# Hi products first, then lo products, in the merged up groups of a split-precision MLP

## The chip, the cores and the metric

The kernel runs on one core of a Trainium2 chip. The metric is device time in microseconds for one execution; lower is better. Before the change the median of three runs is 1174.59 us (1173.49 to 1175.37).

## The reference, cut to what matters

One decoder layer over 256 tokens with a width of 2048, all in float32: modulated norm, combined projection, two kinds of attention and a convolution, output projection, then the MLP, which is the part that the change touches:

```python
h = rms_norm(x, norm2_g[l]) * (1.0 + sc2) + sh2
x = x + g2 * (jnp.square(jax.nn.relu(h @ w_mlp1[l])) @ w_mlp2[l])   # 2048 -> 8192 -> 2048
return rms_norm(x, final_g)
```

## The kernel before

Every large product is computed from two parts of each operand: a rounded copy (hi, type fp32r) and what is left of it (lo). For `h @ w` three products are summed: hi x hi, hi x lo, lo x hi. The weights come from memory as float32 blocks (`raw`, four buffers, 1 MB each, two "halves" in a block). For each half of 128 x 1024 weights, the scalar engine (ACT) writes the rounded copy into `w_hi[j % 4]` (`weight_hi`, line 893) and counts `hi_done`; the vector engine (DVE) subtracts it from the raw weights into `w_lo[j % 4]` (`weight_lo`, line 1850) and counts `lo_done`; TensorE (PE) multiplies the half and counts `pe_half` at its last product. SyncE refills a raw block once `lo_done` says that it was used. The cast of half j waits for `pe_half` of half j - 4, because there are four buffers.

The activations of the MLP's first matrix, h, lie in `act_both` (line 319) as 16 blocks of 128 features, each with 256 tokens of hi and then 256 tokens of lo.

The MLP goes through four quarters of the 8192 hidden features. The first quarter's first matrix is done with three narrow products (`feature_rows`, lines 1275 to 1277). In quarters 1, 2 and 3 it is done by `up_group` and `merged_rows` (lines 1280 to 1311): four groups a quarter, 512 hidden features each, over 8 halves. A half has two blocks of 128 input features (kk) and four tiles of 128 hidden features (m), each tile with a PSUM bank of its own in `quad[par]`. For each kk and m there is one *wide* product (line 1285: 128 weight columns of w_hi, and hi and lo of the activations side by side, 512 columns) and one *narrow* product (line 1287: w_lo with the hi activations, 256 columns, added to the first half of the same bank). So a half has 8 wide and 8 narrow products in turn, and in the whole kernel there are 12 groups, 96 halves and 768 of each. The groups of a quarter are run by a loop of two passes over two groups (`mlp_up`, line 1798), in which thresholds of waits depend on the loop's register.

Each quarter then has four down groups (`down_group`, `split_group`), in which the weights are the moving operand of 512 columns (`token_rows`, lines 1299 to 1301), and some halves of which (`split_half`, lines 1329 to 1357) are replaced by 21 narrow products with waits for sums of weights and activations.

Of the kernel before, what the change touches and what calls it, by code (L numbers as in the profile page):

```python
# [7 lines left out]
P = 128  # L8
D = 2048
S = 256  # L10
TT = S // P
KT = D // P
# [12 lines left out]
GW = 512  # L25
# [6 lines left out]
HALVES = 8  # L32
# [207 lines left out]
def build(nc, x_d, c_d, wmod_d, bcol_d, bmod_d, n1_d, n2_d, fg_d, main_d, tail_d, bf_d, wck_d, wcv_d, pos_d,  # L240
# [7 lines left out]
    with ctx:  # L248
        def sb(name, shape, dt=f32, where=ctx):
            return where.enter_context(nc.sbuf_tensor(name, shape, dt))  # L250

        def sem(name):
            return ctx.enter_context(nc.semaphore(name))
# [3 lines left out]
        w_hi = [sb(f"w_hi{i}", [P, 2 * GW], f32r) for i in range(4)]  # L257
        w_lo = [sb(f"w_lo{i}", [P, 2 * GW], f32r) for i in range(4)]
# [56 lines left out]
        def in_hold(name, start, shape, dt=f32):  # L315
            return nc.alloc_sbuf_tensor_at(name, shape, dt, offset=hold_at + start)

        K = 1024
        act_both = in_hold("act", 0, [P, KT, 2, S], f32r)
        act_hi, act_lo = act_both[:, :, 0, :], act_both[:, :, 1, :]  # L320
# [92 lines left out]
        quad = [ctx.enter_context(nc.psum_tensor(f"quad{i}", [P, 4 * GW], f32)) for i in range(2)]  # L413
# [20 lines left out]
        hi_done = sem("hi_done")  # L434
        lo_done = sem("lo_done")
        pe_half = sem("pe_half")
# [828 lines left out]
        def _(pe):  # L1265
            mm = nc.tensor.matmul
# [10 lines left out]
                    last = mm(out, lo, act_hi[:, k, :], start=False, stop=end, skip_group_check=True)  # L1277
                return last

            def merged_rows(par, j, k, kk, begin, end):  # L1280

                for m in range(4):
                    out = quad[par][:, m * GW:(m + 1) * GW]
                    cols = slice(kk * GW + m * P, kk * GW + (m + 1) * P)
                    mm(out, w_hi[j % 4][:, cols], act_both[:, k, :, :].rearrange("p h t -> p (h t)"),  # L1285
                       start=begin, stop=False, skip_group_check=True)
                    last = mm(out[:, 0:S], w_lo[j % 4][:, cols], act_hi[:, k, :], start=False, stop=end,  # L1287
                              skip_group_check=True)
                return last

            def token_rows(par, j, k, kk, a_hi, a_lo, begin, end, width=GW, tiles=range(TT), weights=None):
# [12 lines left out]
            def up_group(g, par):  # L1304

                for j in range(HALVES):
                    pe.wait_ge(lo_done, g * 8 + (j + 1))
                    for kk in range(2):
                        k = 2 * j + kk
                        last = merged_rows(par, j, k, kk, k == 0, k == KT - 1)  # L1310
                    last.then_inc(pe_half, 1)

            def down_group(q, cg, gates=False):

# [105 lines left out]
            for k in range(KT):  # L1420
                one = mm(quad[0][:, k * P:(k + 1) * P], c_act[:, k:k + 1].to_broadcast([P, P]), ident[:, :],
                         start=True, stop=True)
# [200 lines left out]
            for slot, (half, step) in enumerate(SLOTS):  # L1623
# [42 lines left out]
                if slot == NSA_SLOT + 3:  # L1666
                    pe.wait_ge(cmp_sb, 2)
                    for g in range(NKV):
                        last = nc.tensor.transpose(spare[:, P + g * HD:P + (g + 1) * HD], v_cmp_t[:, g, :],
                                                   ident[0:HD, 0:HD])  # L1670
# [5 lines left out]
                if slot in (NSA_SLOT + 11, NSA_SLOT + 12):  # L1676
# [4 lines left out]
                    for g in range(NKV):  # L1681
                        last = nc.tensor.transpose(
                            spare[:, g * P:(g + 1) * P],
                            p_cmp[:, tt, 4 * g:4 * g + 4, :].rearrange("p h n -> p (h n)"), ident[:, :])
# [113 lines left out]
            def mlp_up(q):  # L1798
                with pe.Fori(0, 2) as i:
                    for par in range(2):  # L1800

                        pe.wait_ge(evac_dve, q * 4 + (3 + par))
                        pe.wait_ge(up_used, q * 4 + i * 2 + (par - 1))
                        up_group(q * 8 + i * 2 + (G_MLP + par), par)
# [861 lines left out]
```

## Time and profile before

| | |
|---|---|
| median of 3 runs | 1174.59 us |
| span of the profiled execution | 1172.2 us |
| TensorE busy | 1134.7 us, 97% |
| VectorE busy | 983.7 us, 84% |
| ScalarE busy | 641.5 us, 55% |
| wide products, line 1285 | 768 |
| narrow products of merged groups, line 1287 | 768 |
| DMA | 314.65 MB, mean 268 GB/s |

The profile is one execution; its span is 2.4 us below the median of the runs. Products of TensorE overlap in the trace, and a product's listed duration is from its start to its modelled end; the time that one takes of the engine is the distance from its start to the next start. Starts are given to 10 ns.

### The profile page before, as it was taken

To read this page: it belongs to the slowest core of one execution; us is meant where nothing else is said; L and a number is where in the kernel's file an instruction comes from. 1 tells how busy PE (TensorE), PEld (TensorE's weight loads), DVE (VectorE), ACT (ScalarE), POOL (GpSimd) and SP (SyncE) were. 2 spreads that over 40 slices of the span, in tenths; PEclk is the share of its full clock that TensorE was granted. 3 is DMA by queue.
4 is the path that set the end of the run, shared out by engine and by line. 5 is a ranking of instruction groups with operands and counts; after the bars stand their busy time and mean duration, and the time that the engine had idled before them with its cause. 6 is when DMAs were issued, how large, how long until landed. Compare 5 with 4: busy or idle time off the path is not lost.

```text
span 1172.2 us, 17842 instructions
## 1 busy us (share of the span) xinstructions
PE 1134.7 (97%) x7087; PEld 1005.2 (86%) x7087; DVE 983.7 (84%) x1182; ACT 641.5 (55%) x936; POOL 23.6 (2%) x40
## 2 busy tenths in 40 slices
PE   4999999999999999999999999999999999999996
PEld 4899989999887778999788888888888888888885
DVE  5998989988997988997887788987778987878774
ACT  6655458877775546544454445554455544445452
POOL 1000000100000000010000000000000000000000
PEclk6999999999999999999999999999999999999999
DMA  9999998878966897985657675657674667666451
GB/s 372 420 420 420 421 409 310 255 205 281 358 227 249 301 304 292 401 351 183 210 186 266 240 282 180 215 187 277 238 270 176 218 202 263 251 231 262 152 180 72
DMA packets 48322, 314.65 MB, mean 268 GB/s; under 512 B 6572, under 2 KB 8440, under 8 KB 11768
## 3 DMA queue, kind: packets, MB, share of 16 engines
q1 hardware_dynamic: 44592, 305.72, 70.1%
q0 software_dynamic: 1760, 5.26, 2.4%
q10 hardware_dynamic: 1896, 2.64, 0.8%
q8 instruction: 51, 0.84, 0.3%
q14 instruction: 23, 0.19, 0.0%
HBM read 305.20 MB, written 4.21 MB: 264 GB/s over the span
## 4 chain that ended last, share of the span: by engine, by line
PE 76%; DVE 11%; DMA 5%; ACT 4%; issue 3%; SPq 0%; ACTq 0%; DVEq 0%
PE quad L1285 15%; PE quad L1299 10%; PE quad L1300 10%; PE quad L1301 10%; PE quad L1287 8%; PE quad L1275 5%; PE quad L1276 5%; PE quad L1277 5%; DMA first_raw<-in_w_mod 3%; DVE w_lo L1850 3%; PE quad L1346 2%; PE quad L1345 2%; PE quad L1347 2%; DVE mod_raw L1857 2%; DMA mod_raw<-in_w_mod 2%
## 5 line engine op out<-in xcount | busy, mean ns | idle before, releaser
L893 ACT ACTIVATE w_hi<-raw 128x1024 fp32r<-128x1024 f32 (+1 forms) x342 | 355.4, 1044 | 304.9 <-PE quad L1301 115.9
L1850 DVE TENSOR_TENSOR w_lo<-raw,w_hi 128x1024 fp32r<-128x1024 f32 (+1 forms) x342 | 408.3, 1204 | 112.4 <-ACT w_hi L893 110.4
L1285 PE MATMUL quad<-act,w_hi 128*128 128x512 f32 x768 | 266.4, 390 | 0.0
L1275 PE MATMUL quad<-act,w_hi 128*128 128x256 f32 x760 | 215.2, 283 | 6.0 <-DVE w_lo L1850 3.9
L1287 PE MATMUL quad<-act,w_lo 128*128 128x256 f32 x768 | 216.6, 282 | 0.0
L1276 PE MATMUL quad<-act,w_hi 128*128 128x256 f32 x760 | 213.1, 280 | 0.0
L1277 PE MATMUL quad<-act,w_lo 128*128 128x256 f32 x760 | 213.1, 280 | 0.0
L1285 PEld LDWEIGHTS quad<-act,w_hi 128*128 128x128 f32 x768 | 144.2, 188 | 30.2
L1275 PEld LDWEIGHTS quad<-act,w_hi 128*128 128x128 f32 x760 | 144.1, 190 | 8.7 <-issue 4.6
L1299 PE MATMUL quad<-w_hi,u_hi 128*128 128x512 f32 x376 | 148.8, 396 | 0.6 <-DVE u_lo L2307 0.6
L1301 PE MATMUL quad<-w_hi,u_lo 128*128 128x512 f32 x376 | 148.7, 396 | 0.0
L1300 PE MATMUL quad<-w_lo,u_hi 128*128 128x512 f32 x376 | 148.7, 396 | 0.0
L1287 PEld LDWEIGHTS quad<-act,w_lo 128*128 128x128 f32 x768 | 145.1, 189 | 0.1
L1276 PEld LDWEIGHTS quad<-act,w_hi 128*128 128x128 f32 x760 | 144.1, 190 | 0.2
L1277 PEld LDWEIGHTS quad<-act,w_lo 128*128 128x128 f32 x760 | 144.0, 189 | 0.0
L1857 DVE CUSTOM_DVE_ANT_0 mod_raw<-mod_raw,acc 128x2048 f32<-128x2048 f32 x36 | 82.1, 2285 | 11.0 <-ACT acc L869 8.0
L1301 PEld LDWEIGHTS quad<-w_hi,u_lo 128*128 128x128 f32 x376 | 70.6, 188 | 17.0
L1299 PEld LDWEIGHTS quad<-w_hi,u_hi 128*128 128x128 f32 x376 | 70.6, 188 | 16.8 <-DVE u_lo L2307 1.2
L1300 PEld LDWEIGHTS quad<-w_lo,u_hi 128*128 128x128 f32 x376 | 70.6, 188 | 15.4
L1868 DVE SCALAR_TENSOR_TENSOR acc<-mod_raw,c_act,acc 128x2048 f32<-128x2048 f32 x31 | 72.7, 2346 | 0.2 <-DMA acc<-in_b_mod 0.2
L983 ACT ACTIVATE score<-score,neg_max 128x128 f32<-128x128 f32 x72 | 31.9, 444 | 40.8 <-DVE neg_max L1989 40.8
L900 ACT ACTIVATE w_hi<-raw 128x768 fp32r<-128x768 f32 x30 | 25.4, 847 | 47.2 <-PE quad L1347 24.2
(371 smaller groups left out, 1715.6 us busy)
## 6 DMA issues: line engine op xcount, KB each, us to landing
raw<-in_w_main SPq DMA_DIRECT2D x184, 1024.0 KB, 5.0
mod_raw<-in_w_mod SPq DMA_DIRECT2D x67, 1024.0 KB, 7.2
first_raw<-in_w_mod SPq DMA_DIRECT2D x14, 1024.0 KB, 15.3
late_raw<-in_w_mod SPq DMA_DIRECT2D x10, 1024.0 KB, 7.9
acc<-in_w_mod SPq DMA_DIRECT2D x4, 1024.0 KB, 12.5
conv_b<-conv_q POOLq DMA_DIRECT2D x8, 512.0 KB, 5.2
x_a<-in_x SPq DMA_DIRECT2D x2, 1024.0 KB, 7.2
x_scratch<-x SPq DMA_DIRECT2D x1, 2048.0 KB, 11.7
```

Source lines behind the costliest of these rows:

```text
L893: A(dst[:, 0:2 * width], block_half(raw, j, width), ACT.Copy).then_inc(hi_done, 1)
L1275: mm(out, hi, act_hi[:, k, :], start=begin and m % 2 == 0, stop=False, skip_group_check=True)
L1276: mm(out, hi, act_lo[:, k, :], start=False, stop=False, skip_group_check=True)
L1277: last = mm(out, lo, act_hi[:, k, :], start=False, stop=end, skip_group_check=True)
L1285: mm(out, w_hi[j % 4][:, cols], act_both[:, k, :, :].rearrange("p h t -> p (h t)"), start=begin, stop=False, skip_group_check=True)
L1287: last = mm(out[:, 0:S], w_lo[j % 4][:, cols], act_hi[:, k, :], start=False, stop=end, skip_group_check=True)
L1299: mm(out, t_hi, hi, start=begin, stop=False, skip_group_check=True)
L1300: mm(out, t_hi, lo, start=False, stop=False, skip_group_check=True)
L1301: last = mm(out, t_lo, hi, start=False, stop=end, skip_group_check=True)
L1850: TTn(lo[:, 0:2 * width], block_half(raw, j, width), hi[:, 0:2 * width].bitcast(f32), ALU.subtract)\
L1857: v.tensor_tensor_reduce(out=src[:, :], in0=src[:, :], in1=acc[0][:, :], scale=1.0, scalar=0.0, op0=ALU.mult, op1=ALU.add, accum_out=m_col ...
L1868: STT(out, src[:, :], c_act[:, bass.ds(k, 1)], out, ALU.mult, ALU.add).then_inc(mod_step, 1)
```

## The change

Within a half of a merged group, the eight wide products are issued first, in the order of kk and m, and then the eight narrow ones in the same order. The wide ones wait for `hi_done` of the half, the narrow ones for `lo_done`. The `start` flag stays with the wide products of the first kk of the first half, `stop` with the narrow ones of the last kk of the last. `pe_half` is still counted at the last product of the half. No buffer and no other engine's code is changed.

```diff
-            def merged_rows(par, j, k, kk, begin, end):
-
-                for m in range(4):
-                    out = quad[par][:, m * GW:(m + 1) * GW]
-                    cols = slice(kk * GW + m * P, kk * GW + (m + 1) * P)
-                    mm(out, w_hi[j % 4][:, cols], act_both[:, k, :, :].rearrange("p h t -> p (h t)"),
-                       start=begin, stop=False, skip_group_check=True)
-                    last = mm(out[:, 0:S], w_lo[j % 4][:, cols], act_hi[:, k, :], start=False, stop=end,
-                              skip_group_check=True)
+            def merged_rows(g, par, j):
+
+                halves = [(kk, m, slice(kk * GW + m * P, kk * GW + (m + 1) * P)) for kk in range(2) for m in range(4)]
+                pe.wait_ge(hi_done, g * 8 + (j + 1))
+                for kk, m, cols in halves:
+                    mm(quad[par][:, m * GW:(m + 1) * GW], w_hi[j % 4][:, cols],
+                       act_both[:, 2 * j + kk, :, :].rearrange("p h t -> p (h t)"), start=j == kk == 0, stop=False,
+                       skip_group_check=True)
+                pe.wait_ge(lo_done, g * 8 + (j + 1))
+                for kk, m, cols in halves:
+                    last = mm(quad[par][:, m * GW:m * GW + S], w_lo[j % 4][:, cols], act_hi[:, 2 * j + kk, :],
+                              start=False, stop=j == HALVES - 1 and kk == 1, skip_group_check=True)
                 return last
@@
             def up_group(g, par):
 
                 for j in range(HALVES):
-                    pe.wait_ge(lo_done, g * 8 + (j + 1))
-                    for kk in range(2):
-                        k = 2 * j + kk
-                        last = merged_rows(par, j, k, kk, k == 0, k == KT - 1)
-                    last.then_inc(pe_half, 1)
+                    merged_rows(g, par, j).then_inc(pe_half, 1)
```

## Rows read from the trace of the kernel before

**Rows 1.** Page: span, TensorE's busy time and share, granted clock in 40 slices.
```profile
span 1172.2 us, 17842 instructions
PE 1134.7 (97%) x7087; PEld 1005.2 (86%) x7087; DVE 983.7 (84%) x1182; ACT 641.5 (55%) x936; POOL 23.6 (2%) x40
...
PEclk6999999999999999999999999999999999999999
```

**Rows 2.** Groups by line, TensorE: shapes, count, busy us, mean ns, idle before.
```profile
L1285 PE MATMUL quad<-act,w_hi 128*128 128x512 f32 x768 | 266.4, 390 | 0.0
L1287 PE MATMUL quad<-act,w_lo 128*128 128x256 f32 x768 | 216.6, 282 | 0.0
L1275 PE MATMUL quad<-act,w_hi 128*128 128x256 f32 x760 | 215.2, 283 | 6.0 <-DVE w_lo L1850 3.9 <-DVE act L1905 2.1
...
L1299 PE MATMUL quad<-w_hi,u_hi 128*128 128x512 f32 x376 | 148.8, 396 | 0.6 <-DVE u_lo L2307 0.6
```

**Rows 3.** Waits of TensorE: who for whom, us in total, times, longest.
```profile
PE quad L1434 <- ACT x_a L879: 11.2, 1, 11.2
PE quad L1275 <- DVE w_lo L1850: 3.9, 3, 1.4
```

**Rows 4.** Windows of two merged stretches: length, busy us (x instructions), clock, DMA.
```profile
633.96:722.71 88.75, 88.75 (x514) 78.67 (x512) 72.17 (x71) 41.97 (x42) 0.00 (x0) 1.00 0.69 252
...
983.11:1071.86 88.75, 88.75 (x514) 78.67 (x513) 71.22 (x54) 41.15 (x39) 0.00 (x0) 1.00 0.67 245
```

**Rows 5.** Timeline, TensorE, first merged stretch: start us, us, line, operation.
```profile
633.96 0.39 PE L1285 MATMUL quad<-act,w_hi 128*128 128x512 f32 x1
...
636.62 0.28 PE L1287 MATMUL quad<-act,w_lo 128*128 128x256 f32 x1
636.74 0.39 PE L1285 MATMUL quad<-act,w_hi 128*128 128x512 f32 x1
...
722.71 0.40 PE L1299 MATMUL quad<-w_hi,u_hi 128*128 128x512 f32 x1
```

**Rows 6.** Timeline, three engines: w_lo made, typical and tightest, and its half's start.
```profile
657.50 1.23 DVE L1850 TENSOR_TENSOR w_lo<-raw,w_hi 128x1024 fp32r<-128x1024 f32 x1 [1.61 <-ACT w_hi L893]
...
668.86 1.04 ACT L893 ACTIVATE w_hi<-raw 128x1024 fp32r<-128x1024 f32 x1
...
669.34 1.22 DVE L1850 TENSOR_TENSOR w_lo<-raw,w_hi 128x1024 fp32r<-128x1024 f32 x1
...
672.79 0.39 PE L1285 MATMUL quad<-act,w_hi 128*128 128x512 f32 x1
```

**Rows 7.** Timeline, TensorE: first of 288 narrow products in a run, and what follows.
```profile
54.32 0.28 PE L1275 MATMUL quad<-act,w_hi 128*128 128x256 f32 x1
...
87.92 0.24 PE L1299 MATMUL quad<-w_hi,act 128*128 128x176 f32 x1
```

**Rows 8.** Timeline, TensorE: runs of wide products, 216 from the first row, then 24.
```profile
1090.52 0.40 PE L1299 MATMUL quad<-w_hi,u_hi 128*128 128x512 f32 x1
...
1140.92 0.40 PE L1299 MATMUL quad<-end_hi,u_hi 128*128 128x512 f32 x1
...
1146.36 0.40 PE L1299 MATMUL quad<-w_hi,u_hi 128*128 128x512 f32 x1
```

**Rows 9.** Timeline, TensorE: first of a split half's 21 narrow products, and what follows.
```profile
725.50 0.28 PE L1345 MATMUL quad<-w_hi,u_hi 128*128 128x256 f32 x1
...
728.00 0.40 PE L1299 MATMUL quad<-w_hi,u_hi 128*128 128x512 f32 x1
```

**Rows 10.** Timeline, TensorE's weight loads (PEld) in a merged half.
```profile
634.31 0.19 PEld L1287 LDWEIGHTS quad<-act,w_lo 128*128 128x128 f32 x1
634.54 0.19 PEld L1285 LDWEIGHTS quad<-act,w_hi 128*128 128x128 f32 x1
```

**Rows 11.** Windows with a low and a full granted clock, columns as in rows 4.
```profile
26.00:34.00 8.00, 7.90 (x47) 7.91 (x48) 7.38 (x7) 5.20 (x7) 0.00 (x0) 0.66 1.02 424
54.32:87.92 33.60, 33.60 (x289) 33.60 (x288) 31.99 (x35) 18.44 (x23) 0.00 (x0) 1.00 1.01 420
```

## The prediction, made before the changed kernel was run

> **What bounds the kernel now.** I read the page's head first: TensorE (PE) is busy 1134.7 of 1172.2 us and its granted clock is full (level 9, 2.4 GHz) in every slice but the first [rows 1]. Then the groups by line, to see which products the change touches: 768 wide ones (line 1285, 512 columns) and 768 narrow ones (line 1287, 256 columns), with 0.0 us of idle time before either [rows 2]. The means in that view, 390 and 282 ns, are not what a product costs: the products overlap in the trace, so I take the time from one start to the next. The waits of the engine say the same as the groups: what TensorE waits for is elsewhere (11.2 us for x at the start, 3.9 us for w_lo, but at line 1275, the projection's narrow products), and no wait at lines 1285 or 1287 is listed [rows 3]. The windows show that the merged groups fill three stretches of the same length, 88.75 us each, at a granted clock of 1.00, TensorE busy throughout [rows 4]. So in the stretches that the change touches, the end is set by the pace at which TensorE takes its products, and by nothing that feeds it.
>
> **The present pace.** The first stretch begins with the wide product at 633.96 and the down group after it begins at 722.71 [rows 5]: 32 halves in 88.75 us, 2.773 us a half, 8 pairs in each, so 346.7 ns a pair. The starts inside it lie about 227 ns (wide to narrow) and 119.5 ns (narrow to wide) apart, averaged over the 768 pairs, with an uncertainty of 1 to 2 ns in the split between the two, since starts are given to 10 ns; their sum is exact. At a half's border, where the present wait for w_lo stands, the step from 636.62 to 636.74 is 120 ns [rows 5], the same as elsewhere: a wait that is already met costs nothing visible.
>
> **Part one, the earlier start on the hi copy: 0 us.** The wide products of a half now wait for hi_done alone. That pays only where w_lo is what comes last. I set the end of each of the 96 w_lo subtractions beside the start of its half. The tightest is that of the half which starts at 672.79: its w_hi is cast from 668.86 for 1.04 us, its w_lo is made from 669.34 to 670.56, after the vector engine had been held by u_lo and the sums, and it is still 2.23 us early [rows 6]. A typical one is made from 657.50 to 658.73 for the half that starts at 664.47 (633.96 + 11 x 2.773), 5.7 us early [rows 5, 6]; the median of the 96 is 5.5 us. The reason is the ring of four weight buffers: the cast of half j may start when half j - 4 has been multiplied, three halves (8.3 us) ahead of its use. With nothing waited for, nothing is gained. The release of a buffer (pe_half) still comes with the last product of a half, so the scalar engine's casts, the vector engine's subtractions, SyncE's refills behind lo_done and the PSUM evacuations keep their times to within what the pace changes. No DMA is moved past another.
>
> **Part two, the added wait: 0 us, bound +4.8 us.** Each half now has two waits instead of one, 96 more, each with a threshold worked out from the loop's register; behind the second one stand the eight narrow products, the only thing queued, and then the scalar engine waiting for pe_half. The w_lo it asks for is there by at least 2.23 us plus the eight wide products [rows 6]. The trace of before has no wait between two products of a merged half. The nearest rows are the split halves of the down groups: 21 narrow products with two waits more than a plain half, 725.50 to 728.00, 2.50 us [rows 9], against 21 x 116.7 = 2.45 us at the pace of a pure narrow run (below). The excess of 0.05 us, if it were all the waits' and all here, is 96 x 0.05 = 4.8 us. I take 0, since the border step [rows 5] is the same instruction in the same loop and shows none; 4.8 us stays as the bound. Below nothing it can't go: a wait gives no time back.
>
> **Part three, the order itself.** Of the 16 steps in a half, 14 now lie inside a run of equals (7 wide to wide, 7 narrow to narrow); one wide to narrow and one narrow to wide stay. The weight loads keep their number: each product has its own 128 columns before and after.
> - Narrow in a run: the projection's feature rows are the same instruction (256 columns of act, weights from w_hi or w_lo). 288 of them from 54.32 to 87.92 [rows 7] give 116.67 ns, 2.8 ns less than the 119.5 of a narrow one followed by a wide one.
> - Wide in a run: two rates are in the trace. 216 products with w_hi or w_lo as the moving operand, 1090.52 to 1140.92, take 233.3 ns each; the 24 that follow, to 1146.36, with end_hi and end_lo moving, take 226.7 ns [rows 8]. The buffers of the fast ones lie in the memory called hold, and so does act_both, which is the moving operand here; and the present wide step is about 227 ns as well. So I take 227 and keep 233.3 as the upper bound.
> - Sum: 7 x (119.5 - 116.67) = 20 ns a half, 96 halves: **-1.9 us**. With 233.3 for the wide ones: 7 x (233.3 - 227.2) = 43 ns more a half, +4.1 us, in sum +2.2 us, or +4.1 us if the narrow ones gain nothing.
>
> The weight load was checked as a limit: in a pair the load starts with the preceding product (634.31 and 634.54) and shows 0.19 us, longer than a narrow step [rows 10]. But the feature rows load under narrow products without end and hold 116.67 ns, so a load that has only a narrow product above it is no new limit.
>
> The sum is made against the profiled span of 1172.2 us; the median of the runs is 1174.59, 2.4 us above it, and I take the difference as unchanged: 1174.59 - 1.9 = 1172.7 us.
>
> **The rivals.**
> 1. *Order makes no difference.* The 119.5 and 227 may be one cost of 346.7 split at a shifted start: if a narrow product costs 116.67 everywhere, the wide one costs 230.0, which the 10 ns grid of starts doesn't exclude for its cost, and runs of each add up to the same pair. Against it: the wide rows in a run at 226.7 [rows 8]. Time 1174.6 us. The Trainium skill (TensorE: Matmul & The Clock Gate, "Back-to-back issue gap") gives a spacing that depends on the columns alone, N/2.4 + 2.5 ns, 325 ns for a pair in either order; the trace's 346.7 ns is not that figure, but the rule that the order is free speaks for this rival.
> 2. *Wide runs go at the slow rate* of [rows 8]: +2.2 us (1176.8), up to +4.1 (1178.7). For it: most wide products of this kernel run at 233.3. It decides from a wide step of 230 ns on.
> 3. *The second wait is exposed* (slower): TensorE's sequencer has to work out and pass a threshold in the middle of a half, and its products stop for it. Place: line by line between the wide and the narrow run of all 96 halves; price up to 0.05 us each [rows 9], so +4.8 - 1.9 = +2.9 us, 1177.5 us. It decides once it costs more than 20 ns a half.
> 4. *Bank cycling stirs the clock.* Now each bank gets a wide and a narrow product before the next bank; afterwards the bank changes with every product. At the granted clock of 0.66 the products of 26 to 34 us took 8.00 / 47 = 170 ns instead of 116.67 [rows 7, 11]; one up group of 22.2 us at that rate would cost 10 us (1183). Against it: TensorE has no idle time in these stretches, and the clock is 1.00 in all of them [rows 4]. The Trainium skill (same page, "A second HAM failure mode: psum-queue depth-cycling") tells of such a kernel whose engine idled between groups while it cycled through banks.
> 5. *The change does not do what it says*, that is the hi copy alone never lets a product start earlier. That is what I forecast; its opposite, w_lo late somewhere in these groups, would be a gain of the wait removed, and the longest wait for w_lo anywhere is inside 3.9 us in sum [rows 3], none of it here.
>
> **How the numbers follow.** Run-to-run spread is about 1 us, and 0.2% (2.35 us) is about what a measurement can tell from no change. Chances: my forecast 0.42; rival 1, 0.26; rival 2, 0.14; rival 3, 0.12; rival 4, 0.02; a larger gain than worked out (both steps shorter in a run than any row shows) 0.04. Faster by over 0.2% needs less than 1172.2: a good third of my forecast's spread (0.16) and the larger gain (0.04), in sum 0.20. Slower by over 0.2% needs more than 1176.9: half of rival 2 (0.08), most of rival 3 (0.10) and rival 4 (0.02), in sum 0.20. Within: 0.60. The range runs from 1170.8 (forecast less a run's spread) to 1178.5 (rivals 2 and 3 but for their last us) and leaves out rival 4, the larger gain and the two in sum.
>
> **What would show it.** In the profile of after: the three stretches last 32 x 2.753 = 88.1 us instead of 88.75; in a timeline of TensorE, wide starts 227 ns and narrow starts 117 ns apart; no idle time before either line; the w_lo margins as now. Wrong in step three if the wide starts lie 230 or 233 ns apart or the narrow ones still 119.5; wrong in step two if there is a gap between the last wide and the first narrow product, or at the loop's turn after every second group; wrong in step one if the stretches shrink by more than 0.7 us while the steps stay as they are.

## The result, and the profile after

The changed kernel takes 1175.76 us (median of 20 runs, 1175.05 to 1180.12) against 1174.33 us (median of 20, 1172.45 to 1176.09). The ratio is 1.0018, 95% interval [1.0011, 1.0025]: slower by some 2 us (the medians lie 1.4 us apart, the means 2.1), where 1.9 us faster was forecast. The time lies inside the forecast's range of 1170.8 to 1178.5, but on the other side of before. The page's head reads like that of [rows 1]; TensorE is again busy nearly throughout.

```profile
span 1173.7 us, 17842 instructions
...
PE 1135.4 (97%) x7087; PEld 1000.7 (85%) x7087; DVE 983.9 (84%) x1182; ACT 641.3 (55%) x936; POOL 23.5 (2%) x40
```

The windows of the three merged stretches, columns as in [rows 4]:

```profile
632.91:722.51 89.60, 89.60 (x513) 77.84 (x512) 72.22 (x71) 41.98 (x42) 0.00 (x0) 1.00 0.69 249
808.34:897.94 89.60, 89.60 (x513) 77.85 (x512) 72.22 (x71) 41.97 (x42) 0.00 (x0) 1.00 0.69 249
983.77:1073.37 89.60, 89.60 (x514) 77.84 (x512) 71.30 (x54) 41.16 (x39) 0.00 (x0) 1.00 0.66 243
```

Each is 89.60 us long where it was 88.75 [rows 4], so 3 x 0.85 = 2.55 us are lost there. The down groups between the first two keep 85.8 us (722.51 to 808.34; before 722.71, the last row of [rows 5], to 808.53). The first merged product starts 1.05 us earlier (632.91 against 633.96), a difference of the stages ahead of it that the change doesn't touch, in one execution of each kernel. Together that is the 1.5 us between the two spans.

The timeline of TensorE at the start of the first stretch; a row with x8 is a run of eight, and what it costs is the step to the next row:

```profile
632.91 2.03 PE L1285 MATMUL quad<-act,w_hi 128*128 128x512 f32 x8
634.78 1.09 PE L1290 MATMUL quad<-act,w_lo 128*128 128x256 f32 x8
635.71 2.03 PE L1285 MATMUL quad<-act,w_hi 128*128 128x512 f32 x8
637.58 1.09 PE L1290 MATMUL quad<-act,w_lo 128*128 128x256 f32 x8
638.51 0.40 PE L1285 MATMUL quad<-act,w_hi 128*128 128x512 f32 x1
```

A half takes 2.80 us: eight wide in 1.87 (233.7 ns each), eight narrow in 0.93 (116.3 ns); the means over all 768 of each are 233.3 and 116.7 ns. There is no gap between the runs, nor at the loop's turns: every half of the three stretches has the same 2.80 us. The groups by line say the same of waits as [rows 2]:

```profile
L1285 PE MATMUL quad<-act,w_hi 128*128 128x512 f32 x768 | 194.8, 395 | 0.0
...
L1290 PE MATMUL quad<-act,w_lo 128*128 128x256 f32 x768 | 105.2, 279 | 0.0
```

No idle time stands before either line. The mean durations read 395 and 279 ns where [rows 2] had 390 and 282: wide products became 5 ns longer, narrow ones 3 ns shorter. The steps, which are what counts, went from 228.3 to 233.3 ns for the wide and from 118.3 to 116.7 ns for the narrow ones (means over the 768 of each). (The busy sums are smaller only because products of one line in a row overlap.)

### The profile page after: what moved, and what is told of

Its sections match the earlier page's. It is cut to its first block, busy times and chain, and to the rows that moved or that the text cites. A ratio compares the mean times of both kernels' runs of the same rounds, so it can differ in the third digit from the quotient of the medians.

```text
span 1173.7 us, 17842 instructions
## 1 busy us (share of the span) xinstructions
PE 1135.4 (97%) x7087; PEld 1000.7 (85%) x7087; DVE 983.9 (84%) x1182; ACT 641.3 (55%) x936; POOL 23.5 (2%) x40
## 4 chain that ended last, share of the span: by engine, by line
PE 78%; DVE 10%; DMA 5%; ACT 4%; issue 3%; SPq 0%; ACTq 0%; DVEq 0%
PE quad L1285 15%; PE quad L1302 10%; PE quad L1304 10%; PE quad L1303 10%; PE quad L1290 8%; PE quad L1275 5%; PE quad L1277 5%; PE quad L1276 5%; DMA first_raw<-in_w_mod 3%; DVE w_lo L1849 3%; PE quad L1345 2%; PE quad L1346 2%; PE quad L1344 2%; DMA mod_raw<-in_w_mod 2%; DVE mod_raw L1856 2%
## 5 line engine op out<-in xcount | busy, mean ns | idle before, releaser
L1277 PE MATMUL quad<-act,w_lo 128*128 128x256 f32 x760 | 212.0, 279 | 0.0
L1285 PE MATMUL quad<-act,w_hi 128*128 128x512 f32 x768 | 194.8, 395 | 0.0
L1285 PEld LDWEIGHTS quad<-act,w_hi 128*128 128x128 f32 x768 | 137.2, 188 | 26.8
L1275 PEld LDWEIGHTS quad<-act,w_hi 128*128 128x128 f32 x760 | 142.9, 188 | 10.6 <-issue 4.9
L1276 PEld LDWEIGHTS quad<-act,w_hi 128*128 128x128 f32 x760 | 142.9, 188 | 0.2
L1277 PEld LDWEIGHTS quad<-act,w_lo 128*128 128x128 f32 x760 | 142.8, 188 | 0.0
L1290 PEld LDWEIGHTS quad<-act,w_lo 128*128 128x128 f32 x768 | 103.5, 188 | 8.7
L1290 PE MATMUL quad<-act,w_lo 128*128 128x256 f32 x768 | 105.2, 279 | 0.0
```

Of the source, the lines that this page charges most:

```text
L1275: mm(out, hi, act_hi[:, k, :], start=begin and m % 2 == 0, stop=False, skip_group_check=True)
L1276: mm(out, hi, act_lo[:, k, :], start=False, stop=False, skip_group_check=True)
L1285: mm(quad[par][:, m * GW:(m + 1) * GW], w_hi[j % 4][:, cols], act_both[:, 2 * j + kk, :, :].rearrange("p h t -> p (h t)"), start=j == kk = ...
L1290: last = mm(quad[par][:, m * GW:m * GW + S], w_lo[j % 4][:, cols], act_hi[:, 2 * j + kk, :], start=False, stop=j == HALVES - 1 and kk == 1 ...
```

## Experiments: is it the order or the wait?

Two kernels take the change apart; in both, `wide` and `narrow` are the two products of `merged_rows` as functions of their own. The first keeps the order of before and has the two waits:

```diff
                 for j in range(HALVES):
-                    pe.wait_ge(lo_done, g * 8 + (j + 1))
+                    pe.wait_ge(hi_done, g * 8 + (j + 1))
...
+                        for m in range(4):
+                            wide(par, j, kk, m)
+                            if kk == m == 0:
+                                pe.wait_ge(lo_done, g * 8 + (j + 1))
+                            last = narrow(par, j, kk, m)
```

> The kernel before with its order of products kept and the wait split as in the change: the first wide product of a half waits for the hi copy alone, the first narrow one for w_lo. If the order alone costs the time, the three merged stretches stay at 88.75 us and the ratio to before is 1.000 (within 0.1%). If the second wait costs it, each stretch is 89.6 us and the ratio 1.002.

The second has the order of the change and the one wait of before (the diff is against the kernel before):

```diff
                     pe.wait_ge(lo_done, g * 8 + (j + 1))
                     for kk in range(2):
-                        k = 2 * j + kk
-                        last = merged_rows(par, j, k, kk, k == 0, k == KT - 1)
+                        for m in range(4):
+                            wide(par, j, kk, m)
+                    for kk in range(2):
+                        for m in range(4):
+                            last = narrow(par, j, kk, m)
```

> The change's order (eight wide, then eight narrow) with the single wait for w_lo at the head of the half, as before. If the order alone costs the time: stretches of 89.60 us, ratio 1.002, as the change. If the second wait costs it: 88.75 us and 1.000.

Pairs with two waits: 1173.20 us, ratio 0.9992 [0.9980, 1.0004]. Runs with one wait: 1176.27 us, ratio 1.0015 [1.0005, 1.0026]. The windows of the first merged stretch, of the one and then of the other:

```profile
633.00:721.75 88.75, 88.75 (x513) 78.67 (x512) 72.17 (x71) 41.99 (x42) 0.00 (x0) 1.00 0.68 252
```

```profile
635.96:725.56 89.60, 89.60 (x513) 77.87 (x512) 72.22 (x71) 41.97 (x42) 0.00 (x0) 1.00 0.69 250
```

The 96 added waits cost nothing that shows, and waiting for the hi copy alone brings nothing: all three stretches of each kernel have the length of their order, 88.75 or 89.60 us, whatever the waits. The order costs all of the 2.55 us.

## Experiments: what about the order?

> The kernel before, with the sixteen products of a merged half in different orders: in each pass of the loop, the eight halves of the first group are two each in pairs (as before), in runs of 2, in runs of 4, and shifted (W0 W1 N0 W2 N1 ... N7, so that a narrow product follows the wide one of the next bank); those of the second group two each in runs of 8 (as in the change), narrow before wide in each pair, pairs of a wide product with the narrow one of the other block of the same bank, and pairs. The wait for w_lo stays at the head of each half. Every order comes six times or more in the profile, so each has its own time for a half. Known: pairs 2.773 us, runs of eight 2.800. Theory A (what counts is only that a product is followed by one of the other length, each pair of such borders giving 3.3 ns): runs of 2 2.787, runs of 4 2.793, shifted, narrow first and other block 2.773. Theory B (the narrow product gains by following the wide one into the same PSUM bank): runs of 2 and 4 and shifted 2.800, other block 2.773, narrow first 2.800. Theory C (it gains by reading the activations that the wide one has just read): other block 2.800, shifted about 2.777, runs of 2 2.787, narrow first 2.800. Rival, the added wait: all orders here have one wait, so runs of eight would take 2.773.

```diff
+            ORDERS = [[in_runs(1)] * 2 + [in_runs(2)] * 2 + [in_runs(4)] * 2 + [shifted()] * 2,
+                      [in_runs(8)] * 2 + [narrow_first()] * 2 + [other_block()] * 2 + [in_runs(1)] * 2]
...
                 for j in range(HALVES):
                     pe.wait_ge(lo_done, g * 8 + (j + 1))
+                    for what, kk, m in ORDERS[par][j]:
+                        last = (wide if what == "W" else narrow)(par, j, kk, m)
```

Time of a half, worked out from the starts of the records (in ns, mean of the six times that each comes), first and second half of the same order:

```
pairs        2774  2773        runs of 8      2800  2800
runs of 2    2786  2773        narrow first   2772  2773
runs of 4    2791  2800        other block    2792  2773
shifted      2793  2793        pairs          2773  2773
```

None of the three theories holds. The first and the second half of one order differ. For the other block this may be the border alone, since its first half follows a wide product. But runs of 2 and runs of 4 follow a narrow product both times, so the time isn't a sum of what each product costs after its neighbour; it depends on more of what came before. Runs of eight take 2800 ns with one wait, so the rival is out here too. In the timeline a half of runs of 2 shows the short pattern, one of runs of 4 the long one:

```profile
644.18 0.62 PE L1283 MATMUL quad<-act,w_hi 128*128 128x512 f32 x2
644.64 0.40 PE L1290 MATMUL quad<-act,w_lo 128*128 128x256 f32 x2
...
646.95 1.08 PE L1283 MATMUL quad<-act,w_hi 128*128 128x512 f32 x4
...
649.74 1.09 PE L1283 MATMUL quad<-act,w_hi 128*128 128x512 f32 x4
...
652.54 0.63 PE L1283 MATMUL quad<-act,w_hi 128*128 128x512 f32 x2
```

From 644.18 to 646.95 are 2.77 us, from 649.74 to 652.54 2.80 us. A pair in the short pattern has steps of 228.3 and 118.3 ns, in sum 346.7; in runs they are 233.3 and 116.7. Once it has settled, which takes up to some ten products, each pattern repeats itself (233.3 is the mean of steps of 230 to 235 ns that recur in the same order).

> The up groups of three quarters computed with other products, so their results are left out; each half of the ring has one kind of sequence and is read from the profile by itself, per product or pair. First group of a pass: 16 wide in a run; 8 wide with w_lo as weights, then 8 narrow with w_hi; pairs with w_hi for both; pairs whose narrow product reads the lo activations; pairs whose narrow product adds to the second half of the bank; 16 narrow, w_hi and w_lo in turn. Second group: pairs of 384 and 256 columns; pairs of 512 and 128; 16 wide into one bank; 16 wide with w_hi and w_lo in turn, two to a bank; 16 narrow into one bank; 16 of 384 columns. Theory A (lengths alone): the two single-length kinds cost 233.3 or 116.7 ns a product whatever the weights and banks, all mixed pairs of 512 and 256 cost 346.7. Theory B (same bank): pairs into the second half of the bank, and one-bank runs, differ from the rest. Theory C (same data just read): pairs with the lo activations cost 350. Theory D (a wide product is faster while w_lo rather than w_hi is being loaded under it): wide in a run with w_lo as weights 227, wide with w_hi and w_lo in turn 230, pairs with w_hi for both 350.

Steps between starts, settled, in ns:

```
16 wide, w_hi                     233.3   pairs, w_hi for both               346.7
8 wide w_lo, then 8 narrow w_hi   233.3, 116.7
16 wide, w_hi and w_lo in turn    233.3   pairs, narrow reads lo             346.7
16 wide into one bank             233.3   pairs, narrow into second half     346.7
16 narrow, w_hi and w_lo          116.7   16 narrow into one bank            116.7
pairs of 512 and 128              282 and 58   16 of 384 columns             177
pairs of 384 and 256              291 a pair, not settled in one half
```

Theories B, C and D of this run fall. Its theory A stands as far as it goes: in these sequences, which copy the weights are from, which bank is written and whether the narrow product reads hi or lo make no difference once the steps have settled, only the sequence of lengths does. But it leaves the 226.7 ns of [rows 8] unexplained: those wide products are in a run, too.

## Experiments: where the buffers lie

What the fast rows of [rows 8] have of their own is where the operands lie. Two large allocations hold them: `arena` has u_hi and u_lo, `hold` has act_both and later end_hi and end_lo (copies of weights for the last group). In each partition, the kernel before has w_hi from byte 49280, u_hi from 122272 and act_both (and end_hi) from 192416. From w_hi to u_hi is 32 modulo 256, from w_hi to act_both too, from u_hi to end_hi 0; the tiles within them begin at multiples of 512. Taken as the start of the moving operand less that of the 128 stationary columns (here called the weights, whatever they hold), modulo 256, that is 32 for the merged and the projection's narrow products, 224 for the down groups (w_hi moves over u), and 0 for end_hi over u. This number is called the distance below. Three kernels shift groups of buffers by 32 bytes (`shift_a` ahead of arena, `shift_w` ahead of raw):

```diff
+        sb("shift_w", [P, 8])
         raw = [sb(f"raw{i}", [P, 4 * GW]) for i in range(4)]
...
+        sb("shift_a", [P, 8])
         arena = sb("arena", [P, ARENA // 4])
```

> The kernel before with 32 unused bytes put ahead of arena and hold, so that act_both, u_hi, u_lo and the end buffers start at a multiple of 64 bytes, as w_hi and w_lo do (before, they start 32 bytes past one). Theory P (the pace of products depends on how the starts of the moving operand and of the weights loaded under it lie to each other): the down groups, at 233.3 ns a wide product before, go to about 227 as the last groups with end_hi did, and the merged pairs may change too. Rival Q (placement plays no part, the pace is a matter of the sequence of products alone): every stretch keeps its rate, merged stretches 88.75 us, down groups 233.3 ns.

> The kernel before with 32 unused bytes ahead of the raw buffers, which moves all later ones: w_hi and w_lo then start 32 bytes past a multiple of 64, and act_both, u and end at a multiple. Theory P: a mirror image of before, so merged pairs 346.7 ns, down groups 233.3; if it is the moving operand's own start that counts, the down groups go to 227 and the merged ones change. Rival Q: nothing changes.

> The kernel before with 32 unused bytes ahead of the raw buffers and 32 more ahead of arena: all buffers of products start 32 bytes past a multiple of 64. Theory P (it counts that both lie alike): as with 32 bytes ahead of arena alone. Rival Q: nothing changes, merged stretches 88.75 us, down groups 233.3 ns.

With `shift_w` alone the distances stay as they were, and so do the rates: 88.75 us a stretch and 233.3 ns in the down groups, at 1173.02 us. With `shift_a`, alone or with the other, the distance in the merged groups is 64, and both kernels give 90.44 us a stretch (353.3 ns a pair), at 1179.98 and 1178.40 us. (Each of these times is one execution, beside 1174.40 us for one of before; the readings rest on the stretches.) The first stretch of the kernel with `shift_a` alone:

```profile
635.54:725.98 90.44, 90.44 (x513) 78.78 (x512) 72.33 (x71) 41.97 (x42) 0.00 (x0) 1.00 0.68 248
```

So placement counts, the rival Q is out, and what counts is the distance and not the start of either. The down groups stayed at 233.3 ns in all three: where the shift changed their distance, from 224 to 192, it was no cure, against what I had expected of the first of the three. Two sweeps then took the distance alone:

```diff
+            def swept(par, j, kk, m, lo):
+                off = (2 * j + kk) * GW - (GW if (j, kk) == (HALVES - 1, 1) else 0) + 8 * (par * HALVES + j)
...
+                return mm(quad[par][:, m * GW:(m + 1) * GW], w_hi[j % 4][:, cols], act_all[:, off:off + GW],
+                          start=j == kk == 0, stop=False, skip_group_check=True)
```

> The merged groups with the order of before, but each of the sixteen halves of a pass (two groups of eight) reads its moving activations from a start that is 32 bytes later than in the half before it (0, 32, ... 480 bytes), so the products are of other data and the result is left out. The distance from the weight buffers to the moving operand is 288 bytes modulo 512 at offset 0. Theory P (the distance between the moving operand and the weights loaded under it sets the pace): 346.7 ns a pair at offset 0, 353.3 at offset 32 (as measured with arena moved by 32), and some value of its own at each other offset, best at offset 224, where the distance is a multiple of 512 as it is for end_hi under u. Rival Q (offset 32 was slow because of the other buffers): 346.7 throughout.

> The same sweep of the moving operand's start in 32 byte steps, with the order of the change: eight wide, then eight narrow. The result is left out here too. Theory P: 350 ns for a wide and a narrow one at offset 0; at offset 224 (distance a multiple of 512) the wide ones take 226.7 to 227.3 ns in a run, as the last groups with end_hi do, and there the order of the change is no worse than pairs. Rival (the order costs 3.3 ns a pair wherever the buffers lie): runs are slower than pairs at every offset.

Time of a half in ns by the distance from weights to moving operand, modulo 256 (each distance comes at two places of the sweep, offsets 0 to 224 and 256 to 480, six times at each; the two places agree within 3 ns but for the two marked, whose halves begin after other sequences):

```
distance   32    64    96   128   160   192   224     0
pairs    2782* 2804  2801  2803  2783  2818  2813  2828
runs     2802  2772* 2818  2808  2821  2799  2806  2780
```

(\*: 2778 and 2779 at the other place.) The period is 256 bytes. Pairs are the better order at 32, 96, 128 and 160, runs at 64, 192, 224 and 0. The change met a distance of 32. Of pairs I had expected 353.3 ns at 64 and the best time at 0; a half at 64 gives 2804 / 8 = 350.5 ns a pair, and 0 is the slowest. The wide products of runs at 0 do come to 226.7 ns, but only from the fourth of the eight on.

A half of sixteen products is too short to settle, so these are not the rates of whole stretches: pairs at 64 take 2804 ns here and 2826 in the stretch of 90.44 us above, and the last six products of the half already show its pace (230 + 118 + 233 + 124 + 236 + 119 ns, 353.3 a pair). The sweep shows that distance and order matter together; which order wins in a long stretch is tested below at 0 and above at 32, and elsewhere it is open. Two halves from the timelines, at distance 0 and then 32, with pairs:

```profile
653.96 0.39 PE L1289 MATMUL quad<-act,w_hi 128*128 128x512 f32 x1
...
656.79 0.40 PE L1289 MATMUL quad<-act,w_hi 128*128 128x512 f32 x1
...
659.57 0.39 PE L1289 MATMUL quad<-act,w_hi 128*128 128x512 f32 x1
```

and with runs:

```profile
651.93 1.99 PE L1289 MATMUL quad<-act,w_hi 128*128 128x512 f32 x8
...
654.71 2.03 PE L1289 MATMUL quad<-act,w_hi 128*128 128x512 f32 x8
...
657.51 1.99 PE L1289 MATMUL quad<-act,w_hi 128*128 128x512 f32 x8
```

2.83 and 2.78 us with pairs, 2.78 and 2.80 us with runs: the order that wins at one distance loses at the other.

Whole kernels with all three groups of buffers at distance 0 put this to the test, one with the order of before and one with that of the change:

```diff
+        neg_max = sb("neg_max", [P, 72])
         raw = [sb(f"raw{i}", [P, 4 * GW]) for i in range(4)]
...
-        neg_max = sb("neg_max", [P, 72])
```

> The kernel before with one small tensor (neg_max, 288 bytes a partition) allocated ahead of the raw buffers instead of after them: w_hi and w_lo come to lie a multiple of 512 bytes from u_hi, u_lo, act and end. Nothing else differs. Theory P: the wide products of the down groups (1089 steps at 233.3 ns after 470 us) go to about 227.3, 6.5 us, the projection's and the output's wide ones may add 2 us, the merged pairs are at most 346.7; some 1165 us. Rival Q: 1174, as before.

> The change with the same placement. Theory P: wide in a run 227, narrow 116.7 ns, merged stretches of 32 x 8 x 344 ns = 88.1 us, no slower than pairs in the same placement. Rival (order costs wherever the buffers lie): 2 us slower than the aligned kernel with pairs.

Pairs: 1175.82 us, ratio to before 1.0019 [1.0007, 1.0031]. Runs: 1173.26 us, ratio 0.9990 [0.9979, 1.0002]. Their first stretches:

```profile
633.63:724.07 90.44, 90.44 (x513) 78.50 (x512) 72.33 (x71) 41.97 (x42) 0.00 (x0) 1.00 0.68 248
```

```profile
634.94:724.30 89.36, 89.36 (x513) 78.68 (x512) 72.20 (x71) 42.01 (x42) 0.00 (x0) 1.00 0.68 251
```

The same edit is now worth 3 x 1.08 = 3.2 us in the stretches, to the good. The down groups went from 233.3 to 227.6 ns as expected, but the projection's narrow products from 116.7 to about 120, which I had left out of the sum, and the merged pairs, which I had put at 346.7 at most, took 353.3, 5.1 us more over the three stretches. So neither kernel gained the 8 us hoped for. And runs didn't reach the 88.1 us that I had expected: wide ones come to 227 only late in a run (230.0 on average), and narrow ones are at 119 and not at 116.7.

The last kernel picks the distance for each kind: 0 from w_hi to arena, for the down groups, and 32 to act_both, for the projection and the merged pairs. Beside `neg_max` ahead of the raw buffers, as above, its edit is:

```diff
         arena = sb("arena", [P, ARENA // 4])
+        sb("shift_h", [P, 8])
         hold = sb("hold", [P, 2 * KT * S])
-        arena_at, hold_at = nc.sbuf_base - ARENA - 8 * KT * S, nc.sbuf_base - 8 * KT * S
+        arena_at, hold_at = nc.sbuf_base - ARENA - 32 - 8 * KT * S, nc.sbuf_base - 8 * KT * S
```

> The kernel before, order of pairs, with two distances chosen instead of one: neg_max ahead of the raw buffers, so that arena (u_hi, u_lo, the output's operands) lies a multiple of 512 bytes from w_hi and w_lo, and 32 unused bytes between arena and hold, so that act_both lies 32 bytes modulo 256 from them, as before. Theory P: merged stretches 88.75 us as before, the projection's narrow products 116.8 ns as before (aligned_pairs had 90.44 and 120.1), the down groups' wide ones 227.6 ns as in aligned_pairs (before 233.3), split halves 119.6 (before 118.5); 1088 x 5.7 = 6.2 us less, 600 x 1.1 = 0.7 us more, some 1 to 2 us less in the output projection: 1167 to 1169 us, ratio 0.995. Rival Q (the rates belong to something else that the aligned kernels changed): at least one of the two kinds keeps the rate it has in the other kernel, 1174 us or more.

It takes 1168.23 us (median of 5, 1166.91 to 1168.80), ratio 0.9945 [0.9931, 0.9958], inside the 1167 to 1169 expected: faster than the kernels before and after, with neg_max placed elsewhere and 32 unused bytes as the whole edit. Its page's span, its first merged stretch, and the 216 wide products that answer to [rows 8]:

```profile
span 1166.8 us, 17842 instructions
```

```profile
632.42:721.19 88.77, 88.77 (x514) 78.68 (x513) 72.16 (x71) 41.98 (x42) 0.00 (x0) 1.00 0.70 252
```

```profile
1086.49 0.39 PE L1300 MATMUL quad<-w_hi,u_hi 128*128 128x512 f32 x1
...
1135.48 0.40 PE L1300 MATMUL quad<-end_hi,u_hi 128*128 128x512 f32 x1
```

48.99 us for 216 are 226.8 ns, before 233.3. The 48 products with end_hi and end_lo, whose distance to u is now 32, went the other way, from 227.3 to 233.5 ns: the same products on the same buffers, 32 bytes on.

One rival is left: the weight buffers are also what the scalar and the vector engine write all the while, so the distance might count towards their writes and not towards TensorE's own reads. The end of the kernel before settles it. The last weights are made by 1148.74, and TensorE then multiplies what is there:

```profile
1146.39 2.35 DVE L1850 TENSOR_TENSOR w_lo<-raw,w_hi 128x1024 fp32r<-128x1024 f32 x2
```

```profile
1149.86 0.40 PE L1299 MATMUL quad<-w_hi,u_hi 128*128 128x512 f32 x1
...
1151.26 0.40 PE L1299 MATMUL quad<-w_hi,u_hi 128*128 128x512 f32 x1
...
1151.97 0.39 PE L1299 MATMUL quad<-end_hi,u_hi 128*128 128x512 f32 x1
...
1157.43 0.40 PE L1299 MATMUL quad<-w_hi,u_hi 128*128 128x512 f32 x1
...
1158.83 0.40 PE L1299 MATMUL quad<-w_hi,u_hi 128*128 128x512 f32 x1
```

Six products with w_hi and w_lo take 1.40 us (233.3 ns each) before and after, the 24 with end_hi and end_lo between them 5.46 us (227.5 ns), with no weight buffer being written.

## Why the prediction was wrong, step by step

- **What bounds.** Right. TensorE's own pace sets the end in the three stretches, and the change in it is the change in time: 3 x 0.85 = 2.55 us in the stretches are 0.22%, inside the measured interval of 0.11 to 0.25%.
- **Part one, the earlier start: 0 us.** Right, shown by the kernel with pairs and two waits (88.75 us a stretch). With w_lo ready at least 2.23 us early [rows 6] there was nothing to win. (The cast of 668.86 in [rows 6] is not that half's: it ends at 669.90, after the subtraction of 669.34 began. The half's own cast is the one before it, from 667.10. The 2.23 us don't hang on it.)
- **Part two, the added wait: 0 us.** Right, by the same kernel. The bound of 4.8 us from the split halves [rows 9] was no cost of waits: their products run at 118.5 ns in the kernel before, and with the same waits at 116.6 when arena and hold are moved by 32 bytes and at 119.6 in the aligned kernels.
- **Part three, the order: -1.9 us. This step failed.** It took 227 ns for a wide product in a run, no more than in a pair, and kept 233.3 as the bound; the change runs at 233.3. Its starting point was off as well: the steps of a pair are 228.3 and 118.3 ns in the mean of the 768, where the prediction read 227 and 119.5. So the narrow ones gained 7 x 1.6 = 11 ns a half, or 1.1 us and not 1.9, and the wide ones lost 7 x 5.0 = 35 ns, or 3.4 us and not 4.1; in the difference the misreading drops out. So the sum is that of rival 2, +2.2 us, and the rest up to 2.55 comes from the two borders in each half, which I had left at the price of a pair, 346.7 ns, while a half costs 8 x 350. The choice between the two rows of [rows 8] was made by where the moving operand lies (in hold). That was the wrong property: it is the distance between it and the weights being loaded under it, and end_hi over u_hi has another one (0) than act_both over w_hi (32). What should have warned me: the 227 ns read for a pair (228.3 in truth) and the 227 ns of end_hi had no reason to be the same thing, and of rival 2 I had written that most wide products of this kernel run at 233.3.
- **The weight load as a limit**: that a narrow product above a load is no new limit was right as far as 116.7 ns goes, yet the weights do matter for the pace, through where they lie.
- **The rivals.** Rival 1 (order makes no difference) is out: 2.55 us in the stretches. The formula of the Trainium skill that I set beside it (TensorE: Matmul & The Clock Gate, "Back-to-back issue gap") is given there for an isolated product; of a stream of weight loads and products the same section says that both set the spacing. It is no rule that the order is free, as I took it. A spacing by columns alone is not what the runs show: 512 columns take 226.7 to 236.6 ns a step in the mean, by order and placement. Rival 2 happened. Rival 3 is out by experiment. Rival 4: the granted clock stayed at 1.00 in all three stretches with the bank changing at each product. Rival 5 came as I had forecast: the hi copy alone starts nothing earlier.
- **The chances.** Rival 2 had 0.14 against 0.42 for my forecast. The rows in hand were one for and one against; a fair split would have been even, and with that the sign open. The range held the result through the room left for rivals 2 and 3, not through the forecast. Its lower end is not what it is called, either: 1172.7 less a spread of 1 us is 1171.7, and 1170.8 takes the 1.9 us between the lowest and highest of three runs.

## What to carry to other kernels

When TensorE never waits, an edit that only reorders its products can still change the time: compare the steps between starts, not the durations, of each sequence that the new order makes, and take a rate only from rows whose operands lie at the same distance. If a row with the same shapes has two rates, find out what sets them before choosing one. A sweep of the start address inside one kernel, one offset a half, costs one run and can be worth more than the edit: here 32 unused bytes and one moved tensor gave 0.55%. Such a sweep shows that placement counts, not the rate of a long stretch (2804 against 2826 ns a half at distance 64), so the choice has to be measured in whole kernels.

## What the runs showed of the hardware

- The pace of back-to-back products with a weight load under each depends on the distance between the moving operand and the weights, with a period of 256 bytes: a half of eight wide and eight narrow products takes 2772 to 2828 ns, by distance and order, for the same number and shapes of products. The Trainium skill (TensorE: Matmul & The Clock Gate, "Step-by-step: what each phase is for") says that weights come by a read port of their own and that loading the next tile's steals no read bandwidth from the running product; these runs show that the pace does depend on how the starts of the two operands lie to each other: moving both by 32 bytes changes nothing (88.75 us a stretch), moving one costs 1.69 us a stretch. That it is the load under the running product which meets it is inferred, since no run here has products without loads. Which part of the memory or the engine they meet in, no run here shows either.
- The pace has a memory: after a change of sequence or distance the steps take up to some ten products to settle, and two halves of the same order, both begun after a narrow product, can cost 2786 and 2773 ns (runs of 2). What it is that remembers stays open.
- At a distance of 32, a pair of 512 and 128 columns takes 282 + 58 = 340 ns, nearly as long as one of 512 and 256 (346.7): the shorter product saves almost nothing, the wide one then takes longer.
